# A two-block transformer kernel: masks and softmax factors of the attention moved to TensorE, and the first block run in three passes over the tokens

## The chip, the cores and the metric

The kernel runs on one core of a Trainium2 chip. A core has TensorE (PE, matrix products), VectorE (DVE), ScalarE (ACT), GpSimd (POOL), SyncE (SP), and 16 DMA engines that they share. Times are device microseconds of one execution; lower is better. All data are fp32.

## What is computed

512 tokens (four tiles of 128) of width 1024 go through two blocks. The first has 16 extra meta tokens in front. Cut to what matters here:

```python
h = concatenate([meta, x])                       # 16 + 512 tokens
z = rmsnorm(h) @ w_in                            # latents, retention q k v g, two gates
y_a = mla_branch(...)                            # causal attention, 8 heads, keys of 64+32
y_r = retention_branch(...)                      # chunks of 128 with a carried state
h = h + (sigmoid(za) * y_a + sigmoid(zr) * y_r) @ w_mix_out
# experts: 8 heads x 16 picks of 16384 for each token
act = gelu(einsum('td,tkd->tk', x, peer_u[idx])) # idx from two top-16 lists of 128 keys
h = h + einsum('tk,tkd->td', gates * act, peer_v[idx])
```

The second block has a pooled branch, an attention of 16 heads with three branches for each head (compressed keys, selected keys, window; the last two are plain causal here), a merge of both, and an MLP of width 4096. A score row is masked causally, `p = softmax(s)`; each branch is multiplied by a gate that belongs to the token and head. Where a token sees no compressed key, that branch is zero.

## The kernel before

**Passes.** The first block runs in passes over groups of tiles, `FIRST = ((0, 2), (2, 4))` at line 38: tiles 0 and 1 with the meta tokens, then tiles 2 and 3. The second block runs over `SECOND = ((0, 2), (2, 3), (3, 4))`. Each pass streams all weights of its block from memory through `weight_ring`, three slabs of up to 2 MB, in the order of `weight_plan`; SyncE issues a load as soon as the slab three places earlier has been used. `first_wave` writes the stages of a pass: norm (`n1`), latents (`lat`, `nq`, `nkv`), up-projections (`up`), head norms with rope (`qk`), turns (`tq`, `tk`), attention (`ma`), retention products and stage (`rp`, `tr`, `re`, `rn`), the gated merge (`m1`), output (`mix`), norm (`np`), the experts' queries (`pq`), and for each tile the selection of its experts (`sel0` to `sel3`). With several tiles in a pass, `merge_stage` and `product_stage` compute features by tokens; with one tile, `merge_tile_stage` and `turned_stage` compute tokens by features with 512 columns and turn the result. A slab that serves one tile is 8 products of 512 columns.

**The picks.** `Picks` gathers the expert rows. A step is one pick k of one tile t in one table: 4 tiles x 2 tables x 128 picks = 1024 steps, and each gathers 128 rows of 4 KB from `peer_u` or `peer_v` by an indirect DMA that GpSimd issues (line 315) into one of 8 buffers `picks_rows`. VectorE multiplies a `peer_u` row block with the tokens and sums (line 374), or adds a weighted `peer_v` row block to `h` (line 380). For tile 1, three of four `peer_v` picks are added by TensorE instead, with a diagonal of weights that GpSimd makes (lines 333 and 403). The gathers of tile t can start when its expert numbers are written (line 1465). `SHARES` says how many steps VectorE does within each stage, spread evenly between its own instructions: `g.picks.use(dve)`. The order of all engines is thus fixed when the program is written. A tile's picks must be done before the second block uses the tile (`finish`); `drain_0` takes what is left of tiles 0 and 1. Up to there 512 steps have been done: 24 in `sel1`, 358 in the pass over tiles 2 and 3, 51 each in `sel2` and `sel3`, 28 in the drain.

**Attention.** `attention_stage` works on pairs of items; an item is one head (and branch) of one tile. For a pair s: TensorE computes scores into PSUM (line 863, meta keys at 865); VectorE adds the mask and takes the row's least in one instruction, which also writes the masked scores back to PSUM (line 945, scores are negated); ScalarE takes the exponential and its sum (907); VectorE forms 1/sum (954) and multiplies the probabilities by it and by the gate (956, 958; for compressed keys also by the table `cmp_seen`, 953); TensorE turns each block of 128 keys against the identity (874); ScalarE copies them out (917, 920); TensorE multiplies by the values (885). On TensorE the order is scores of pair s, turns of s - 1, values of s - 2. Each item has its own semaphore counts for `least` and `normed`. In the second block a triple of pairs (compressed, selected, window) serves two heads, so 8 triples a tile.

## Time and profile before

| | |
|---|---|
| median of 3 runs | 3163.65 us (3157.81 to 3178.35) |
| profiled execution | 3159.39 us, of which span 3158.1 us |
| PE busy | 2272.4 us (72%) |
| DVE busy | 1802.2 us (57%) |
| POOL busy | 1432.2 us (45%) |
| ACT busy | 426.0 us (13%) |
| DMA | 829.57 MB, of which 539.99 MB gathered |
| granted TensorE clock, mean | 0.81 |

The page slices the span in 40 parts of 79 us: TensorE's busy share is high in the first 470 us and in the last 500 us, GpSimd's only from 525 to 2750 us, and the DMA engines' share is 0.7 or more from 710 to 2770 us. The shares of busy time are averages over stages with different limits, so the stages are read one by one. TensorE's records are pipelined, so its busy time is not its speed. It runs at one of two clocks, 1.2 or 2.4 GHz; the granted share of a stretch is the mean, 0.50 for all at the lower and 1.00 for all at the higher.

### The profile page before, as it was taken

The numbers are of one execution on the slowest core, as the hardware profiler recorded it, in microseconds if no ns is written. First come the engines' busy times: TensorE is split into PE (matmuls) and PEld (weight loads), VectorE is DVE, ScalarE is ACT, GpSimd is POOL, SyncE is SP. The second block draws the span as 40 slices with busy tenths as digits, with TensorE's granted clock in tenths as the row PEclk, the third lists the DMA queues.
The fourth block names the chain that finished last, engine by engine and source line by source line (L and its number), as shares of the span: only waits on it lengthen the run. The fifth ranks groups of instructions, "written<-read, shape, count | busy, mean of one in ns | idle before, by whom it ended". The sixth has DMA issues, their size and how long they took to land. (4 is left out here: it accounts for less than half of the span.)

```text
span 3158.1 us, 24727 instructions
## 1 busy us (share of the span) xinstructions
PE 2272.4 (72%) x8222; PEld 1376.0 (44%) x8222; DVE 1802.2 (57%) x3876; ACT 426.0 (13%) x1209; POOL 1432.2 (45%) x1137
## 2 busy tenths in 40 slices
PE   5997980056673784767674478979957687969989
PEld 3535850023432662322344235758425443437544
DVE  1512119978779677566477897674666854224300
ACT  1212000011200100000000232012000321013310
POOL 0000002377667787778767764676655433100000
PEclk9796995577695796999885557989977688987999
DMA  3310522599889999978889877999998779942376
GB/s 129 121 67 27 173 96 101 157 350 370 282 337 329 333 401 352 321 237 266 293 306 398 288 249 230 394 386 393 363 360 330 259 246 379 340 153 83 126 259 220
DMA packets 291759, 829.57 MB, mean 263 GB/s; under 512 B 23568, under 2 KB 30016, under 8 KB 290864
## 3 DMA queue, kind: packets, MB, share of 16 engines
q0 software_dynamic: 148464, 539.99, 47.7%
q1 hardware_dynamic: 139872, 283.19, 24.7%
q10 hardware_dynamic: 3296, 4.80, 0.4%
q8 instruction: 66, 1.08, 0.1%
q14 instruction: 61, 0.50, 0.1%
HBM read 825.81 MB, written 2.10 MB: 262 GB/s over the span
## 5 line engine op out<-in xcount | busy, mean ns | idle before, releaser
L315 POOL DMA_INDIRECT picks_rows<-peer_u_dram,expert x512 | 723.5, 1413 | 830.2 <-DVE expert L1465 516.2
L315 POOL DMA_INDIRECT picks_rows<-peer_v_dram,expert x512 | 618.1, 1207 | 477.4 <-DVE h L380 354.6
L374 DVE CUSTOM_DVE_ANT_0 picks_rows<-picks_rows,xn 128x1024 f32<-128x1024 f32 x512 | 613.7, 1223 | 169.0 <-DMA picks_rows<-peer_u_dram,expert 144.4
L380 DVE SCALAR_TENSOR_TENSOR h<-picks_rows,picks_weight,h 128x1024 f32<-128x1024 f32 x416 | 535.0, 1286 | 189.4 <-DMA picks_rows<-peer_v_dram,expert 116.3
L465 PE MATMUL psum<-weight_ring,hnT 128*128 128x512 f32 (+4 forms) x576 | 236.9, 573 | 23.0 <-DMA weight_ring<-w_in_dram 10.9
L403 PE MATMUL psum<-picks_rows,picks_diag 128*128 128x512 f32 x384 | 187.3, 625 | 59.9 <-POOL picks_diag L333 59.5
L1753 PE MATMUL psum<-weight_ring,aT 128*128 128x512 f32 x512 | 220.8, 593 | 3.1 <-ACT aT L2060 1.4
L465 PEld LDWEIGHTS psum<-weight_ring,hnT 128*128 128x128 f32 (+1 forms) x576 | 106.2, 187 | 152.4 <-issue 137.5
L874 PE MATMUL psum<-identity_sb,na_probs 128*128 128x128 f32 (+2 forms) x384 | 93.7, 359 | 100.9 <-DVE na_probs L958 79.4
L656 PE MATMUL psum<-identity_sb,n_scaled 128*128 128x128 f32 (+1 forms) x104 | 24.1, 412 | 181.9 <-DVE n_scaled L640 181.9
L1753 PEld LDWEIGHTS psum<-weight_ring,aT 128*128 128x128 f32 x512 | 96.9, 190 | 125.3 <-issue 120.5
L403 PEld LDWEIGHTS psum<-picks_rows,picks_diag 128*128 128x128 f32 x384 | 67.8, 194 | 178.1 <-issue 176.2
L465 PE MATMUL psum<-weight_ring,mergedT 128*128 128x512 f32 x256 | 117.2, 620 | 20.1 <-DVE mergedT L1216 18.7
L1333 PE MATMUL psum<-weight_ring,xn 128*128 128x512 f32 x256 | 117.1, 613 | 11.2 <-DVE xn L621 7.4
L1181 PE MATMUL psum<-hnT,weight_ring 128*128 128x256 f32 x512 | 116.4, 390 | 5.0 <-ACT xn L1140 5.0
L465 PE MATMUL psum<-xn,weight_ring 128*128 128x256 f32 x512 | 113.2, 385 | 8.6 <-DVE xn L621 8.6
L874 PEld LDWEIGHTS psum<-identity_sb,na_probs 128*128 128x128 f32 (+2 forms) x384 | 48.4, 159 | 161.7 <-DVE na_probs L958 152.4
L907 ACT ACTIVATE na_probs<-psum,na_least 128x15 f32<-128x15 f32 (+6 forms) x192 | 83.7, 441 | 190.9 <-DVE na_least L945 190.8
L1181 PEld LDWEIGHTS psum<-hnT,weight_ring 128*128 128x128 f32 x512 | 100.3, 196 | 20.1 <-ACT xn L1140 5.8
L465 PEld LDWEIGHTS psum<-xn,weight_ring 128*128 128x128 f32 x512 | 98.9, 193 | 22.8 <-issue 8.9
L1770 DVE TENSOR_TENSOR h<-h,psum 128x512 f32<-128x512 f32 x8 | 5.5, 689 | 180.9 <-PE psum L1753 180.9
L945 DVE CUSTOM_DVE_ANT_0 psum<-psum,mask_sb 128x128 f32<-128x128 f32 (+7 forms) x160 | 76.4, 514 | 51.9 <-PE psum L865 31.3
(353 smaller groups left out, 3170.8 us busy)
## 6 DMA issues: line engine op xcount, KB each, us to landing
weight_ring<-w_ff_dram SPq DMA_DIRECT2D x48, 2048.0 KB, 11.0
weight_ring<-w_in_dram SPq DMA_DIRECT2D x44, 2048.0 KB, 13.6
weight_ring<-w_proj_nsa_dram SPq DMA_DIRECT2D x6, 2048.0 KB, 8.1
weight_ring<-w_out_dram SPq DMA_DIRECT2D x6, 2048.0 KB, 14.8
weight_ring<-w_ret_out_dram SPq DMA_DIRECT2D x4, 2048.0 KB, 8.0
weight_ring<-w_mix_out_dram SPq DMA_DIRECT2D x4, 2048.0 KB, 18.9
weight_ring<-w_peer_q_dram SPq DMA_DIRECT2D x4, 2048.0 KB, 13.4
picks_rows<-peer_u_dram,expert POOLq DMA_INDIRECT x512, 7.8
```

What stands on the lines that cost most here:

```text
L315: pool.indirect_dma_start(out=self.rows[:, n % GATHERS, :], out_offset=None, in_=table, in_offset=bass.IndirectOffsetOnAxis(ap=self.expert ...
L374: ins = nc.vector.tensor_tensor_reduce(out=row, in0=row, in1=self.x[t], scale=1.0, scalar=0.0, op0=ALU.mult, op1=ALU.add, accum_out=self.d ...
L380: ins = nc.vector.scalar_tensor_tensor(out=h, in0=row, scalar=self.weight[:, t % 2, k:k + 1], in1=h, op0=ALU.mult, op1=ALU.add)
L403: mm = nc.tensor.matmul(self.g.psum[:, bank, :], self.diag[:, at % DIAGS, :], self.rows[:, n % GATHERS, 512 * c:512 * c + 512], start=(k = ...
L465: mm = g.nc.tensor.matmul(g.psum[0:rows, n % BANKS, 0:cols], lhsT, rhs, start=(k == 0), stop=(k == len(pairs) - 1))
L656: mm = nc.tensor.transpose(g.psum[:, 2 * (t % 2) + c // 4, P * (c % 4):P * (c % 4) + rows], buffer(t)[0:rows, P * c:P * c + P], g.identity ...
L874: mm = nc.tensor.transpose(turned(j, m, keys), probs[:, j % 4, at:at + keys], g.identity[:])
L907: nc.scalar.activation(probs[:, i % 4, 0:items[i].keys], scores(i), ACT.Exp, bias=least[:, i % 8:i % 8 + 1], scale=-1.0, accum_out=rowsum[ ...
L945: nc.vector.tensor_tensor_reduce(out=scores(i), in0=scores(i), in1=items[i].mask, scale=1.0, scalar=-LOWEST, op0=ALU.add, op1=ALU.min, acc ...
L1181: mm = nc.tensor.matmul(g.psum[0:rows, n % BANKS, 0:cols], lhsT, rhs, start=(k == 0), stop=(k == len(pairs) - 1))
L1333: mm = nc.tensor.matmul(g.psum[:, n % 3, :], lhsT, rhs, start=(k == 0), stop=(k == len(pairs) - 1))
L1753: mm = nc.tensor.matmul(g.psum[:, n_tiles * b + t, :], aT[:, KT * k + i, P * t:P * t + P], w[:, i, :], start=(k == 0 and i == 0), stop=(k ...
```

## The change

**The passes.** `FIRST` becomes ((0, 1), (1, 2), (2, 4)). Tile 0 and the meta tokens go alone, then tile 1 alone, then tiles 2 and 3. The weights of the first block are streamed three times. `sel0` ends pass 0, `sel1` pass 1. The shares are 140 steps up to and with `sel1` (121 and 19), 241 in the pass over tiles 2 and 3, 34 and 35 in `sel2` and `sel3`, 62 in the drain. The shares of the second block stay.

**The attention.** The mask is added by TensorE: after both scores of a pair, a product of the identity and the mask of the last 128 keys (the only ones that can be masked) is accumulated in PSUM. VectorE takes the least of both items in one `tensor_reduce` without writing scores back; the reciprocals of the pair are one instruction, the gates another. For items of more than 128 keys VectorE no longer scales the probabilities but writes `turner`, a diagonal of the factors, for both items, and TensorE turns the blocks by a full product with that diagonal in place of the turn against the identity. Items of up to 128 keys are scaled, both in one instruction. `cmp_seen` is replaced by zeroing gates of tile 0 once at the start. The signals `least` and `normed` count pairs, no longer items.

```diff
-FIRST = ((0, 2), (2, 4))
+FIRST = ((0, 1), (1, 2), (2, 4))
 SHARES = {
-    "sel1": 24, "n1_1": 13, "lat_1": 13, "nq_1": 9, "nkv_1": 9, "up_1": 12, "qk_1": 16, "tq_1": 6, "tk_1": 5, "ma2_1": 26,
+    "n1_1": 5, "lat_1": 5, "nq_1": 3, "nkv_1": 3, "up_1": 4, "qk_1": 7, "tq_1": 1, "tk_1": 2, "ma1_1": 10, "rp_1": 13,
...
+        turner = sb("turner", [P, 4, P]) if widest > P else None
...
-                mm = nc.tensor.matmul(scores(i)[:, 0:it.kT.shape[-1]], it.q, it.kT, start=True, stop=True)
+                n = it.kT.shape[-1]
+                nc.tensor.matmul(scores(i)[:, 0:n], it.q, it.kT, start=True, stop=False)
+            for i in pair(s):
+                it = items[i]
+                n, masked = it.kT.shape[-1], it.mask.shape[-1]
+                mm = nc.tensor.matmul(scores(i)[:, n - masked:n], g.identity[:], it.mask, start=False, stop=True)
...
-                pe.wait_ge(*s_normed.after(j + 1))
+                it = items[j]
+                pe.wait_ge(*s_normed.after(s + 1))
...
+                    if it.by_turn:
+                        mm = nc.tensor.matmul(turned(j, m, keys), probs[:, j % 4, at:at + keys], turner[:, j % 4, :], start=True, stop=True)
+                    else:
+                        mm = nc.tensor.transpose(turned(j, m, keys), probs[:, j % 4, at:at + keys], g.identity[:])
...
-                act.wait_ge(*s_least.after(i + 1))
+                act.wait_ge(*s_least.after(s + 1))
...
-                for i in pair(s):
-                    dve.wait_ge(*s_scores.after(i + 1))
-                    nc.vector.tensor_tensor_reduce(out=scores(i), in0=scores(i), in1=items[i].mask, scale=1.0, scalar=-LOWEST,
-                                                   op0=ALU.add, op1=ALU.min, accum_out=least[:, i % 8:i % 8 + 1]).then_inc(s_least.sem, 1)
+                it = items[2 * s]
+                dve.wait_ge(*s_scores.after(2 * s + 2))
+                nc.vector.tensor_reduce(least[:, both(s, 8)], both_scores(s), AX_X, ALU.min).then_inc(s_least.sem, 1)
                 g.picks.use(dve)
...
+                f = factor[:, both(s, 8)]
+                dve.wait_ge(*s_exp.after(2 * s + 2))
+                link(nc.vector.reciprocal(f, rowsum[:, both(s, 8)]))
+                if it.gate is not None:
+                    link(nc.vector.tensor_tensor(f, f, it.gate, ALU.mult))
+                if it.by_turn:
+                    if s >= 2:
+                        dve.wait_ge(*s_turned.after(2 * s - 2))
+                    ins = nc.vector.tensor_tensor(turner[:, both(s, 4), :], g.identity[:].unsqueeze(1).to_broadcast([P, 2, P]),
+                                                  f.unsqueeze(2).to_broadcast([P, 2, P]), ALU.mult)
+                else:
+                    p = probs[:, both(s, 4), 0:it.keys]
+                    ins = nc.vector.tensor_tensor(p, p, f.unsqueeze(2).to_broadcast([P, 2, it.keys]), ALU.mult)
+                ins.then_inc(s_normed.sem, 1)
```

How the rows of the engines move is shown at three places. The first is VectorE where the expert numbers of tile 0 are written (`expert<-`). Before, the selection of tile 1 follows (`sel_best`), with picks (`picks_dots`) already between:

```order
L1465 SCALAR_TENSOR_TENSOR expert<-sel_number 128x128
L1469 TENSOR_REDUCE sel_total<-sel_weight 128x8
L1470 RECIPROCAL sel_inverse<-sel_total 128x8
L1471 TENSOR_TENSOR gates_sb<-sel_weight,sel_inverse 128x128
L1428 MAX sel_best<-psum 128x8 x4
L374 ISA picks_rows,picks_dots<-picks_rows,xn 128x1024
L374 ISA picks_dots 128x1
L1428 MAX sel_best<-psum 128x8 x4
```

Of the change, the same place; it comes at row 175 of VectorE's order in place of row 284:

```order
L1496 SCALAR_TENSOR_TENSOR expert<-sel_number 128x128
L1500 TENSOR_REDUCE sel_total<-sel_weight 128x8
L1501 RECIPROCAL sel_inverse<-sel_total 128x8
L1502 TENSOR_TENSOR gates_sb<-sel_weight,sel_inverse 128x128
L632 MEMSET n_1_sums 128x1
L634 TENSOR_SCALAR n_1_mean<-n_1_sums 128x1
L636 RECIPROCAL n_1_inverse<-n_1_root 128x1
L645 TENSOR_SCALAR n_1_scaled<-h,n_1_inverse 128x1024
L379 ISA picks_rows,picks_dots<-picks_rows,xn 128x1024
```

The whole pass over tile 1, from its norm (`n_1`) on, now stands behind the first expert numbers and among the picks.

The second place is VectorE in the attention of tile 1 in the second block (`na_0`), a pair of 256 keys between picks (the rows that add to `h`). Before:

```order
L945 ISA psum,na_0_least<-psum,mask_sb 128x256
L945 ISA na_0_least 128x1
L945 ISA psum,na_0_least<-psum,mask_sb 128x256
L945 ISA na_0_least 128x1
L380 SCALAR_TENSOR_TENSOR h<-picks_rows,picks_weight,h 128x1024
L954 RECIPROCAL na_0_factor<-na_0_rowsum 128x1
L958 TENSOR_SCALAR na_0_probs<-na_0_probs,na_0_factor,branch_gates_0 128x256
L954 RECIPROCAL na_0_factor<-na_0_rowsum 128x1
L958 TENSOR_SCALAR na_0_probs<-na_0_probs,na_0_factor,branch_gates_0 128x256
```

Of the change:

```order
L973 TENSOR_REDUCE na_0_least<-psum 128x2
L385 SCALAR_TENSOR_TENSOR h<-picks_rows,picks_weight,h 128x1024
L977 RECIPROCAL na_0_factor<-na_0_rowsum 128x2
L979 TENSOR_TENSOR na_0_factor<-na_0_factor,branch_gates_0 128x2
L983 TENSOR_TENSOR na_0_turner<-identity_sb,na_0_factor 128x256
```

Eight instructions of the pair have become four.

The third place is TensorE in the attention of tile 3 (`na_2`), one triple. Before:

```order
L863 MATMUL psum<-nsa_kT_sb,qT_2 128x512 x2
L874 MATMUL psum<-identity_sb,na_2_probs 31x128 x2
L863 MATMUL psum<-nsa_kT_sb,qT_2 128x512 x2
L874 MATMUL psum<-identity_sb,na_2_probs 128x128 x8
L885 MATMUL psum<-na_2_probsT,v_cmp_sb 64x128 x2
L863 MATMUL psum<-k_cmpT_sb,qT_2 128x31 x2
L874 MATMUL psum<-identity_sb,na_2_probs 128x128 x8
L885 MATMUL psum<-na_2_probsT,nsa_kv_sb 64x128 x8
```

Of the change:

```order
L881 MATMUL psum<-nsa_kT_sb,qT_2 128x512 x2
L885 MATMUL psum<-mask_sb,identity_sb 128x128 x2
L898 MATMUL psum<-na_2_turner,na_2_probs 128x128 x8
L911 MATMUL psum<-na_2_probsT,v_cmp_sb 64x128 x2
L881 MATMUL psum<-k_cmpT_sb,qT_2 128x31 x2
L885 MATMUL psum<-cmp_mask_sb,identity_sb 128x31 x2
L898 MATMUL psum<-na_2_turner,na_2_probs 128x128 x8
L911 MATMUL psum<-na_2_probsT,nsa_kv_sb 64x128 x8
```

Each pair has gained two mask products behind its scores, and its eight turns have the same place with another right-hand side (`na_2_turner`).

## Rows read from the trace of the kernel before

**Rows 1.** Instructions on the tile `expert` (duration ns min/median/max, first and last start):

```profile
L315 POOL DMA_INDIRECT picks_rows<-peer_u_dram,expert x512: 933/1494/3326, 524.8 to 2341.0; - x171
```

**Rows 2.** Instructions on the tile `h`, same columns:

```profile
L380 DVE SCALAR_TENSOR_TENSOR h<-picks_rows,picks_weight,h x416: 1268/1283/1512, 800.8 to 2777.2; 128x1024 f32<-128x1024 f32 x139
```

**Rows 3.** VectorE's groups by shape, 1757 to 1942 us (busy us, mean ns):

```profile
L380 DVE SCALAR_TENSOR_TENSOR h<-picks_rows,picks_weight,h 128x1024 f32<-128x1024 f32 x71 | 90.9, 1280 | 0.2 <-issue 0.2
L374 DVE CUSTOM_DVE_ANT_0 picks_rows<-picks_rows,xn 128x1024 f32<-128x1024 f32 x17 | 20.8, 1221 | 3.5 <-DMA picks_rows<-peer_u_dram,expert 3.5
L954 DVE RECIPROCAL na_factor<-na_rowsum 128x1 f32<-128x1 f32 x96 | 14.9, 156 | 1.6 <-ACT na_probs L907 1.6
L945 DVE DVE_READ_ACCUMULATOR2_ANT na_least<- 128x1 f32 x96 | 13.4, 148 | 0.0
L958 DVE TENSOR_SCALAR na_probs<-na_probs,na_factor,branch_gates 128x256 f32<-128x256 f32 x32 | 13.2, 412 | 1.2
L945 DVE CUSTOM_DVE_ANT_0 psum<-psum,mask_sb 128x256 f32<-128x256 f32 x32 | 12.9, 445 | 0.0
...
L374 DVE DVE_READ_ACCUMULATOR2_ANT picks_dots<- 128x1 f32 x17 | 1.4, 82 | 0.0
```

**Rows 4.** Stretches of the first block: length, busy us by engine, granted clock, DMA share, GB/s:

```profile
24.00:121.00 97.00, 84.63 (x269) 45.38 (x270) 43.55 (x94) 13.50 (x33) 0.00 (x0) 0.95 0.36 125
121.00:167.00 46.00, 43.82 (x184) 29.96 (x184) 13.49 (x64) 16.28 (x67) 0.00 (x0) 0.59 0.01 2
167.00:246.00 79.00, 78.40 (x176) 29.00 (x176) 10.25 (x20) 6.45 (x12) 0.00 (x0) 0.98 0.20 67
246.00:300.00 54.00, 37.69 (x176) 28.63 (x176) 17.70 (x60) 12.50 (x37) 0.00 (x0) 0.59 0.11 39
300.00:400.00 100.00, 98.46 (x448) 86.13 (x448) 10.11 (x24) 8.08 (x20) 0.00 (x0) 0.98 0.40 137
400.00:470.00 70.00, 61.38 (x210) 41.18 (x210) 9.99 (x18) 5.32 (x10) 0.00 (x0) 0.90 0.29 100
470.00:525.00 55.00, 1.98 (x32) 1.78 (x32) 52.23 (x208) 1.59 (x2) 0.24 (x1) 0.54 0.03 11
525.00:609.00 84.00, 3.78 (x32) 3.52 (x32) 79.45 (x257) 0.31 (x1) 35.58 (x32) 0.52 0.62 200
609.00:1273.00 664.00, 401.36 (x1431) 268.03 (x1432) 524.34 (x827) 79.78 (x192) 483.19 (x356) 0.74 0.92 339
1273.00:1532.00 259.00, 188.64 (x449) 73.04 (x447) 150.78 (x455) 4.26 (x7) 215.01 (x217) 0.95 0.81 276
```

**Rows 5.** Stretches: merge of tiles 2 and 3, first block; of tile 2, second block:

```profile
1052.00:1153.00 101.00, 100.14 (x448) 87.03 (x448) 63.67 (x116) 7.58 (x18) 73.27 (x52) 0.97 0.98 369
2563.00:2615.00 52.00, 50.91 (x116) 22.25 (x116) 11.95 (x12) 4.16 (x6) 9.68 (x7) 0.96 0.83 304
```

**Rows 6.** Timeline of TensorE, one 2 MB slab for one tile (start us, us):

```profile
2661.47 7.03 PE L1333 MATMUL psum<-weight_ring,xn 128*128 128x512 f32 x16
```

**Rows 7.** Stretches: second block's attention, tiles 0 and 1, tile 2, tile 3:

```profile
1758.00:1942.00 184.00, 117.04 (x576) 61.37 (x576) 171.08 (x520) 63.66 (x297) 117.30 (x92) 0.54 0.81 264
2464.00:2563.00 99.00, 74.19 (x433) 45.68 (x433) 86.33 (x244) 41.79 (x148) 41.11 (x37) 0.74 0.69 213
2876.00:2961.00 85.00, 74.09 (x529) 50.08 (x528) 54.02 (x208) 48.78 (x147) 0.00 (x0) 0.89 0.00 1
```

**Rows 8.** VectorE's reduces by shape, whole span (busy us, mean ns):

```profile
L1464 DVE TENSOR_REDUCE sel_number<-sel_scratch 128x128 f32<-128x2048 f32 x8 | 18.3, 2286 | 0.3
L789 DVE TENSOR_REDUCE qk_head_sums<-qk_head_squares 128x8 f32<-128x768 f32 x8 | 7.6, 953 | 0.3
```

**Rows 9.** Timeline of TensorE in the attention of tile 3 (start us, us):

```profile
2885.37 1.12 PE L874 MATMUL psum<-identity_sb,na_probs 128*128 128x128 f32 x8 [0.50 <-ACT na_probsT L917]
2886.42 1.58 PE L885 MATMUL psum<-na_probsT,nsa_kv_sb 128*64 128x128 f32 x16
2887.93 1.13 PE L863 MATMUL psum<-nsa_kT_sb,qT 64*128 64x512 f32 x4
```

55 lines of the change are left out of this document (27 added, 28 removed), and 12 rows, old and new, of the table SHARES.

## The prediction

> **What bounds the kernel now.** I read first when the instructions on two tiles start and end, then the groups of one engine by shape, then the busy times of stretches. The gathers of expert rows start at 524.8 us and not before, because they wait for the first expert numbers [rows 1]; the last row is added at 2777.2 us [rows 2], and 381 us of tile 3 alone follow. Between lie 1024 gathers, 540 MB in all (0.527 MB each), and VectorE pays 1.22 us (1.30 with the read of its accumulator) for each of `peer_u` and 1.28 us for each of `peer_v` [rows 3]. So the span has three parts: 525 us without gathers, 2252 us with them, 381 us after.
>
> In the first 525 us TensorE is nearly always busy at full clock and the DMA share is 0.01 to 0.40; in the last 55 us VectorE alone picks the experts [rows 4]. In the pass over tiles 2 and 3 (609 to 1273 us) nothing is full alone: VectorE 524 of 664 us, TensorE 401, DMA share 0.92 [rows 4]. In the gating stage of it TensorE has 100 of 101 us and the DMA share is 0.98 at 369 GB/s [rows 5], which I take as the most that the DMA engines give. From 1273 to 1532 us GpSimd is busiest, 215 of 259 us, with the gathers and diagonals of tile 1 [rows 4].
>
> **Part 1: the first block in three passes.** The gathers come earlier, and a third pass over the block's weights is read. By the plan's shapes a pass is 5792 columns of `w_in` at 4 KB plus 16.9 MB of others, 40.6 MB.
>
> The start. Pass 0 now has tile 0 and the 16 meta rows. From [rows 4]: 97 us become 64 (products of a tile or the meta rows against a slab fall from 19 to 11, the norms shrink a little), 46 become 27 (8 of 16 heads), 79 become 50 (7 of 11 products), 54 become 33 (one retention chunk instead of two), 100 become 52 (the same seven slabs' worth in the one-tile form took 52 us [rows 5]; a 2 MB slab is 16 instructions in 7.0 us [rows 6]), 70 become 45, and the selection stays at 55. With the 24 us of loading: 350 us, so the gathers start 175 us earlier. Nothing else uses the DMA then; 40.6 MB in 326 us is 125 GB/s, hidden.
>
> The pass over tile 1. Without picks it would take pass 0's 271 us less the meta rows' products and a meta unit of norms (35 us), 236. It carries 121 picks, 157 us of VectorE at 1.30. How these add I take from the pass of before: without picks, 446 us of pass 0 (24 to 470), less the meta rows, plus the longer attention, about 435; with 358 picks (465 us of VectorE) it took 664. That is 0.74 of the two added. So 0.74 x (236 + 157) = 290 us. The DMA has to move 40.6 + 121 x 0.527 = 104 MB: 282 us at 369 GB/s, 307 at the mean 339 of the pass of before [rows 4]. I take 305, near the DMA's end. Selection of tile 1 with 19 picks instead of 24: 84 - 5 x 1.3 = 77.
>
> The pass over tiles 2 and 3 carries 241 picks: 0.74 x (435 + 313) = 554. Some stages there stand at the gathers' pace and give back all of a removed pick, so I take 545. DMA is no bound: 168 MB, 455 us at 369 GB/s. Then selections 2, 3 and the drain hold 131 picks, 130 before: GpSimd is the bound there, 260 us as before.
>
> Sum: 350 + 305 + 77 + 545 + 260 = 1537 us, against 1532 now: **+5**. The 175 us won at the start, the 7 of a lighter selection and 119 of a lighter pass over tiles 2 and 3 are paid back by 305 of an extra pass.
>
> **Part 2: the attention.** Per pair of heads VectorE had, at 256 keys, 2 x (0.445 + 0.148 + 0.156 + 0.412) = 2.3 us [rows 3]. Now: one reduce over 512 elements, which from 953 ns at 768 and 2286 at 2048 is 1.04 ns an element plus 0.15, 0.68 us [rows 8]; a reciprocal and a product of two columns, 0.16 each; and a diagonal of 128x256, which I price at 0.42 by the scaling of 256 columns. That is 1.42, 0.62 of before. With fewer keys the fixed parts of the eight or ten removed instructions weigh more, and I take 0.52 over all. In the attention of tiles 0 and 1 VectorE has 171 of 184 us [rows 7], 113 of them on picks [rows 3]; so 58 become 30, 28 us less.
>
> TensorE pays for it. In the attention of tile 3 at full clock, 8 blocks are turned in 1.05 us, 16 instructions of values take 1.5 and two heads' scores 1.1 (by the starts of the rows, 1.13 by the last one's own time) [rows 9]: 3.6 us a pair, 8.4 a triple with the compressed pair, of 85/8 = 10.6. A full product of 128 columns takes two instructions of 0.11 (7.03/16 for 512 columns, a quarter [rows 6]), 0.22 us, against 0.13 for a turn. So the masks add 0.44 a pair, the turns as products 0.7 to 0.9, the small pair 0.2: 2.7 us, 11.1 a triple, with the clock already 0.89. VectorE no longer hides anything here (54 of 85 us, no picks). The factor is now also made after both exponentials. 8 x 11.1 = 89 plus 8 for filling and for waits: **97 us, +12**. Bounds: 0 (if only today's idle is used) and +22.
>
> Tiles 0 and 1: VectorE 171 to 143, plus 10 for steps that have no pick between the reduce and the factor, so that the wait for two exponentials shows. TensorE gets 24 us more at full clock, 45 at the granted 0.54, 117 + 45 = 162 [rows 7]. The later of the two with some waits is 169: **-15**; bounds -41 (VectorE alone) and 0. Tile 2: VectorE 86 to about 66, TensorE 74 + 25 = 99 at its clock of 0.74, somewhat less if the clock rises: **-5**, bounds -14 and +5. The first block's attention: less VectorE, more TensorE at a low clock, no net, contained in the passes.
>
> **Sum:** 3159.4 (the profiled execution, 1.3 us more than its span) + 5 + 12 - 15 - 5 = 3156. The profiled execution lies 4 us under the median 3163.65 of the three. I predict 3152, leaning a little to the faster rivals: no change that 1% can tell, and 1% (32 us) is about what a measurement of this kernel tells from no change.
>
> **Rivals.**
> The clock (17%). From 121 to 167 us TensorE is busy 44 of 46 us and yet has 0.59 of its clock, the tiles 0 and 1 attention 0.54 at 117 of 184, the tile 3 attention 0.89 at 74 of 85 [rows 4, 7]. What runs there is short: turns and small products. If replacing turns by products and adding masks lifts the stretches from 1.2 to mostly 2.4 GHz, VectorE bounds tiles 0 and 1 (148 us, -36, where waits shrink too), tile 2 comes to 85 (-14), tile 3 to 95 (+10), and the attention of the first block gives 20: 3159 + 5 - 60 = 3104. The Trainium skill, "TensorE: Matmul & The Clock Gate", Part 4, says that transposes do not count as busy for the gate as matmuls do; by that rule this is what happens. The 0.89 with a quarter of the work in turns neither proves nor excludes it.
>
> Passes that pack better (15%): tile 1 at the DMA's end, 283, and the next pass at 505, because picks hide fully once they are fewer: 3156 - 23 - 40 = 3093.
>
> Passes that pack worse, slower than before (24%): the shares are few per stage, and the one-tile stages are chains. A pick placed between a norm and its drain adds its whole 1.3 us. If a removed pick gives back only what it added on average, (664 - 435)/358 = 0.64 us, the pass over tiles 2 and 3 takes 589 and that over tile 1 313: 3156 + 44 + 8 = 3208. It decides (slower by over 1%) from about 583 us on for the pass over tiles 2 and 3.
>
> The earlier start is nothing (4%): if pass 0 waits for slabs; then its DMA share would be high. The one-tile stretch moved 304 GB/s with TensorE busy 51 of 52 us [rows 5], against it.
>
> The forecast has 40%, its own range 3120 to 3190. Faster by over 1% (under 3132) comes from the first two rivals and a little of the forecast, 0.33; slower (over 3195) 0.24; the rest 0.43. The range 3085 to 3212 takes in the rivals' centres and leaves out about a fifth.
>
> **What would show it.** First gather at 340 to 360 us; expert numbers of tile 1 about 382 us later; tile 1's last pick near 1537; the pass over tiles 2 and 3 between 520 and 570 us; the attention stretches 169, 94 and 97 us, with TensorE's busy time up in all and VectorE's down by a third in the last. Wrong would be a first gather after 400 us, a granted clock over 0.8 in the attention of tiles 0 and 1, or a tile 3 attention under 85 us. A DMA share under 0.8 in the pass over tile 1 would say that its chains bound it, not its bytes.

## The result

| | median | against the kernel before |
|---|---|---|
| kernel before | 3165.26 us (15 runs, 3156 to 3182) | |
| changed kernel | 3192.61 us (15 runs, 3182 to 3209) | 1.009, 95% interval 1.0069 to 1.0111 |

The change costs about 28 us, where 3152 us (0.4% faster) had been forecast. The time is inside the wide range of the prediction (3085 to 3212), but outside the forecast's own 3120 to 3190 and on the wrong side of no change. The profiled executions differ by as much: the span grew from 3158.1 to 3186.3 us. As the change intends, TensorE's busy time rose from 2272.4 to 2382.6 us and VectorE's fell from 1802.2 to 1731.2; the mean granted clock rose from 0.81 to 0.83.

### The profile after

First gather, last pick of the kernel, and the two sums that close tile 1's picks, by tile (duration ns min/median/max, first and last start in us); they answer to [rows 1] and [rows 2]:

```profile
L320 POOL DMA_INDIRECT picks_rows<-peer_u_dram,expert x512: 934/1314/3227, 352.2 to 2344.0; - x171
L385 DVE SCALAR_TENSOR_TENSOR h<-picks_rows,picks_weight,h x416: 1264/1283/1530, 687.7 to 2784.5; 128x1024 f32<-128x1024 f32 x139
L433 DVE TENSOR_TENSOR h<-h,psum x2: 678/682/686, 1551.6 to 1552.2; 128x512 f32<-128x512 f32 x2
```

Before, the last of these rows read:

```profile
L428 DVE TENSOR_TENSOR h<-h,psum x2: 679/684/689, 1541.3 to 1541.9; 128x512 f32<-128x512 f32 x2
```

The gathers start 173 us earlier, and yet tile 1 is complete 10.3 us later. Stretches of the changed kernel, columns as in [rows 4] and [rows 7]: pass 0 up to its attention, what follows that, the selection of tile 0; the pass over tile 1; its selection; the pass over tiles 2 and 3; their selections and the drain; below the gap the first block's attention of tile 0, of tile 1, of tiles 2 and 3, and the second block's of tiles 0 and 1, of tile 2 and of tile 3:

```profile
24.00:87.00 63.00, 49.71 (x147) 24.35 (x147) 25.20 (x59) 8.35 (x21) 0.00 (x0) 0.92 0.52 182
118.00:297.00 179.00, 155.85 (x408) 70.00 (x407) 24.38 (x57) 20.71 (x41) 0.00 (x0) 0.87 0.45 157
297.00:352.00 55.00, 2.06 (x32) 1.86 (x32) 51.88 (x206) 1.88 (x3) 0.00 (x0) 0.54 0.03 10
352.00:652.00 300.00, 200.67 (x573) 105.64 (x574) 182.65 (x346) 39.40 (x95) 168.15 (x126) 0.75 0.94 345
652.00:735.00 83.00, 11.94 (x61) 6.40 (x59) 68.78 (x229) 5.46 (x8) 21.44 (x23) 0.61 0.57 180
735.00:1275.00 540.00, 389.06 (x1505) 262.04 (x1506) 380.79 (x571) 75.93 (x187) 312.82 (x237) 0.82 0.84 301
1275.00:1542.00 267.00, 198.55 (x478) 80.32 (x476) 151.83 (x457) 5.03 (x9) 216.91 (x220) 0.94 0.82 274
...
87.00:118.00 31.00, 27.83 (x113) 17.65 (x114) 4.31 (x13) 8.14 (x34) 0.00 (x0) 0.60 0.06 24
431.00:462.00 31.00, 30.07 (x144) 22.30 (x144) 16.97 (x34) 9.45 (x34) 13.67 (x12) 0.72 0.87 311
866.00:960.00 94.00, 70.89 (x384) 50.76 (x384) 64.24 (x66) 23.59 (x68) 55.72 (x43) 0.85 0.73 253
1773.00:1944.00 171.00, 146.33 (x832) 102.37 (x830) 146.32 (x289) 64.29 (x296) 107.98 (x87) 0.66 0.82 271
2470.00:2573.00 103.00, 89.43 (x625) 67.52 (x626) 73.44 (x132) 42.49 (x147) 37.10 (x37) 0.87 0.65 200
2883.00:2987.00 104.00, 98.12 (x752) 74.52 (x752) 36.66 (x96) 50.24 (x148) 0.00 (x0) 0.97 0.00 1
```

From first to last instruction of each, the second block's attention stages now take 171.6, 102.9 and 103.8 us, against 184.3, 98.8 and 85.1. In every one VectorE works less, TensorE works more and has more of its clock; only the first got shorter. The sum of the three is +10.1, tile 1's end is +10.3, and 7.8 us are spread over stages that the change does not touch.

Timeline of TensorE in tile 3's attention, answering to [rows 9] (start us, us):

```profile
2902.18 1.13 PE L881 MATMUL psum<-nsa_kT_sb,qT 64*128 64x512 f32 x4
2903.24 0.71 PE L885 MATMUL psum<-mask_sb,identity_sb 128*128 128x128 f32 x4
2904.17 2.05 PE L898 MATMUL psum<-na_turner,na_probs 128*128 128x128 f32 x16 [0.22 <-DVE na_turner L983]
2906.15 0.43 PE L911 MATMUL psum<-na_probsT,v_cmp_sb 31*64 31x128 f32 x4
```

The eight turns of a pair, 1.05 us from start to start before, are 16 instructions and 1.98 us (2904.17 to 2906.15).

### The profile page after: what moved, and what is told of

Read it like the earlier page. It is cut to its first block and busy times, and to the rows that moved or that the text cites. A ratio compares the mean times of both kernels' runs of the same rounds, so it can differ in the third digit from the quotient of the medians.

```text
span 3186.3 us, 25522 instructions
## 1 busy us (share of the span) xinstructions
PE 2382.6 (75%) x8814; PEld 1428.5 (45%) x8814; DVE 1731.2 (54%) x3341; ACT 444.4 (14%) x1227; POOL 1399.6 (44%) x1137
## 3 DMA queue, kind: packets, MB, share of 16 engines
q8 instruction: 71, 1.16, 0.1%
## 5 line engine op out<-in xcount | busy, mean ns | idle before, releaser
L320 POOL DMA_INDIRECT picks_rows<-peer_u_dram,expert x512 | 703.7, 1374 | 737.9 <-DVE expert L1496 343.6
L320 POOL DMA_INDIRECT picks_rows<-peer_v_dram,expert x512 | 608.5, 1189 | 609.5 <-DVE h L385 463.8
L661 PEld LDWEIGHTS psum<-identity_sb,n_scaled 128*128 128x128 f32 (+1 forms) x104 | 19.7, 222 | 239.4 <-issue 202.5
L1321 DVE TENSOR_TENSOR m_term<-psum,m_gates 128x512 f32<-128x512 f32 x16 | 11.1, 692 | 193.1 <-PE psum L1293 193.1
L898 PE MATMUL psum<-na_turner,na_probs 128*128 128x128 f32 x576 | 85.7, 304 | 32.3 <-DVE na_turner L983 27.2
L470 PE MATMUL psum<-weight_ring,h2T 128*128 128x512 f32 (+1 forms) x256 | 97.2, 541 | 6.6 <-DVE kc_sb L1566 5.1
L898 PEld LDWEIGHTS psum<-na_turner,na_probs 128*128 128x128 f32 x576 | 75.5, 209 | 39.7 <-DVE na_turner L983 34.2
```

The source lines that it names most:

```text
L320: pool.indirect_dma_start(out=self.rows[:, n % GATHERS, :], out_offset=None, in_=table, in_offset=bass.IndirectOffsetOnAxis(ap=self.expert ...
L470: mm = g.nc.tensor.matmul(g.psum[0:rows, n % BANKS, 0:cols], lhsT, rhs, start=(k == 0), stop=(k == len(pairs) - 1))
L661: mm = nc.tensor.transpose(g.psum[:, 2 * (t % 2) + c // 4, P * (c % 4):P * (c % 4) + rows], buffer(t)[0:rows, P * c:P * c + P], g.identity ...
L898: mm = nc.tensor.matmul(turned(j, m, keys), probs[:, j % 4, at:at + keys], turner[:, j % 4, :], start=True, stop=True)
```

## The experiments

Each ran beside the kernel before on the same chip, and each ratio is to that, with its 95% interval. The number of a kernel is that in its label. Each stage length is read from one profiled execution. The theory after reading the two traces was that both parts of the change lose some 10 us each.

### The two parts alone, and the attention taken apart

Kernel 1 is the changed one with `FIRST` and `SHARES` of before; kernel 2 is the one before with

```diff
-FIRST = ((0, 2), (2, 4))
+FIRST = ((0, 1), (1, 2), (2, 4))
```

and the new shares. Kernels 3 and 4 have two passes, and of the attention only TensorE's mask products with the pair's reduce, or only the diagonals. Both choose in one function, the first line in kernel 3 and the second in kernel 4 (`mask_pe` and `factors` of every stage):

```diff
+    return (True, "each")
```

```diff
+    return (False, "turner")
```

> The two passes and the shares of before, with the whole new attention. Theory (the parts add up, and both lose): the second block's attention moves as in the changed kernel, -13 us for tiles 0 and 1, +4 for tile 2, +19 for tile 3, and the first block's attention by nothing that shows, so +10 us, 3175. Rival 1 (the passes are the loss, and the attention would win on its own): between -10 and 0. Rival 2 (the attention is the whole loss, through the first block too, where two of its three stages stand among picks): +24 to +30, with tile 1's last pick 10 us later than the 1532 us of before.

> The three passes and the shares of the change, with the attention of before. Theory: +10 us at tile 1's last pick (1542), and 3 to 4 more in the second block's first stages, as in the changed kernel, so +12 us, 3177. Rival 1 (passes are the whole loss): +20 to +28. Rival 2 (the new attention is what makes the passes late): 0 to +3, with the last pick of tile 1 at 1532 to 1535.

> The two passes of before; of the attention only TensorE's masks and the one reduce for a pair, while VectorE scales each item as before and the blocks are turned against the identity. By rows, a pair's masks cost TensorE about 0.5 us and VectorE loses 0.5 us of 2.3 at 256 keys. Theory: tiles 0 and 1 -7 us, tile 2 0, tile 3 +7 (8 triples by 0.9 us), sum 0 to +3. Rival (the wait for both scores and both exponentials is the loss, not TensorE's work): tile 3 +12 or more here, and little in the run with the diagonals alone. The clock: if turns against the identity are what keeps the granted clock low, the attention of tiles 0 and 1 stays at 0.54 here; if it is how much TensorE has to do, it rises to about 0.6.

> The two passes of before; of the attention only the diagonals of factors and the full products with them (items of up to 128 keys scaled in one instruction), while VectorE adds the masks and takes the least item by item as before. By rows, the eight turns of a pair take 1.98 us in place of 1.05, 1.9 us for each of 8 triples of tile 3. Theory: tiles 0 and 1 -5 us, tile 2 +3, tile 3 +12, sum +10, so most of the attention's loss is here. Rival (the masks are the loss): tile 3 under +5. The clock: if turns against the identity are what keeps it low, the attention of tiles 0 and 1 rises from 0.54 to 0.66 or more here; if it is how much TensorE has to do, to about 0.6, as with the masks alone.

| kernel | median | ratio | interval | us |
|---|---|---|---|---|
| attention alone | 3204.38 | 1.0118 | 1.0086 to 1.0151 | +37 |
| passes alone | 3155.68 | 0.9967 | 0.9947 to 0.9986 | -10 |
| masks alone | 3178.31 | 1.0034 | 1.0009 to 1.0058 | +11 |
| diagonals alone | 3162.34 | 0.9981 | 0.9962 to 1.0 | -6 |

The theory fell for both parts. The passes gain, and the attention is the whole loss: +37 and -10 make the +28 of the change. It fell for the halves of the attention too: the masks alone cost 11 us where 0 to 3 were expected, and the diagonals alone, expected to be most of the loss at +10, gain 6. The size of the attention's loss surprised, since the second block's stages give only +10. The first stage of the first block, tiles 0 and 1 without any picks, shows the rest. It took 46.3 us before ([rows 4], 121 to 167). With the whole new attention, and below it with the diagonals alone:

```profile
121.00:186.00 65.00, 62.26 (x256) 42.65 (x256) 9.36 (x24) 16.35 (x67) 0.00 (x0) 0.61 0.01 3
```

```profile
119.00:184.00 65.00, 62.25 (x224) 39.95 (x223) 11.52 (x48) 18.02 (x67) 0.00 (x0) 0.52 0.01 2
```

TensorE has 62 of 65 us and little over half of its clock; nothing else is near full. The stage is TensorE's alone, so it has no idle time that would take up added products, and their price goes by the clock that the stage gets. In the changed kernel this is spread over its passes. Beside the passes alone, tile 0's stage goes from 21.9 to 30.3 us, tile 1's from 29.1 to 31.3, tiles 2 and 3's from 86.0 to 94.0: 18.6 us, of which 14.6 arrive where tile 1 is complete, since with the passes alone that comes at 1537.0:

```profile
L430 DVE TENSOR_TENSOR h<-h,psum x2: 680/684/689, 1537.0 to 1537.6; 128x512 f32<-128x512 f32 x2
```

For the second block the two halves of the attention are told apart stage by stage (us, from first to last instruction):

| stage | before | masks alone | diagonals alone | both (changed kernel) |
|---|---|---|---|---|
| tiles 0 and 1 | 184.3 | 178.0 | 175.3 | 171.6 |
| tile 2 | 98.8 | 105.2 | 94.3 | 102.9 |
| tile 3 | 85.1 | 100.0 | 91.5 | 103.8 |

In tile 3 the kernel with the masks loses more, +15 and not the +7 expected; the diagonals lose 6 there and not 12. Timeline of TensorE with the masks alone, and then with the diagonals alone, one triple each; the first rows of each stand one triple apart:

```profile
2895.98 1.58 PE L921 MATMUL psum<-na_probsT,nsa_kv_sb 128*64 128x128 f32 x16
...
2898.55 0.71 PE L895 MATMUL psum<-mask_sb,identity_sb 128*128 128x128 f32 x4
2899.10 1.04 PE L910 MATMUL psum<-identity_sb,na_probs 128*128 128x128 f32 x8
...
2900.77 0.63 PE L895 MATMUL psum<-cmp_mask_sb,identity_sb 128*128 128x31 f32 x4
2902.63 1.12 PE L910 MATMUL psum<-identity_sb,na_probs 128*128 128x128 f32 x8 [1.23 <-ACT na_probsT L953]
...
2907.11 1.58 PE L921 MATMUL psum<-na_probsT,nsa_kv_sb 128*64 128x128 f32 x16
```

```profile
2898.98 1.58 PE L921 MATMUL psum<-na_probsT,nsa_kv_sb 128*64 128x128 f32 x16
...
2901.90 2.05 PE L908 MATMUL psum<-na_turner,na_probs 128*128 128x128 f32 x16 [0.28 <-DVE na_turner L1014]
...
2909.79 1.58 PE L921 MATMUL psum<-na_probsT,nsa_kv_sb 128*64 128x128 f32 x16
```

A triple takes 11.13 us with masks and 10.81 with diagonals. Before, it took 9.51:

```profile
2889.32 1.58 PE L885 MATMUL psum<-na_probsT,nsa_kv_sb 128*64 128x128 f32 x16
...
2894.88 1.12 PE L874 MATMUL psum<-identity_sb,na_probs 128*128 128x128 f32 x8 [1.18 <-ACT na_probsT L917]
...
2898.83 1.58 PE L885 MATMUL psum<-na_probsT,nsa_kv_sb 128*64 128x128 f32 x16
```

So masks add 1.6 us and diagonals 1.3, and the changed kernel has 12.4: the sum. A wait of 1.2 us for ScalarE's copy stands in each triple before, and still stands there with the masks. The copy stands on ScalarE behind the exponentials of the next pair, and these wait for the least, which waits for the scores. The head of this chain, before and then with the masks alone (the scores before start at 2887.93 us [rows 9]):

```profile
2889.09 0.70 DVE L945 CUSTOM_DVE_ANT_0 psum<-psum,mask_sb 128x512 f32<-128x512 f32 x1 [1.84 <-PE psum L863]
2889.89 0.69 ACT L907 ACTIVATE na_probs<-psum,na_least 128x512 f32<-128x512 f32 x1 [2.47 <-DVE na_least L945]
```

```profile
2905.19 1.13 PE L887 MATMUL psum<-nsa_kT_sb,qT 64*128 64x512 f32 x4
2906.99 1.23 DVE L984 TENSOR_REDUCE na_least<-psum 128x2 f32<-128x1024 f32 x1 [2.52 <-PE psum L895]
2908.25 0.69 ACT L943 ACTIVATE na_probs<-psum,na_least 128x512 f32<-128x512 f32 x1 [3.69 <-DVE na_least L984]
```

From the scores to the first least it is 1.80 us in place of 1.16, with the mask products of both items between. From the least to the first exponential it is 1.26 us in place of 0.80, because one reduce now gives the least of both items; before, the exponential of the first item could start while VectorE took the least of the second. The triple has this second step twice in its chain (again 2899.30 to 2900.56, where it was 2892.03 to 2892.81 before). So of the 1.6 us some 0.6 come from the mask products and 0.9 from the common reduce. The rival of kernel 3, that waiting for both items is the loss and not TensorE's work, was right for the larger part of it. No kernel has the masks without the common reduce, so this split is read from one triple and was not tested. The diagonals do fill the wait for the copy (0.28 us of another wait left), which is why 1.9 us more of products cost 1.3.

### Which block, and which stages

Kernel 5 has the new attention in the first block's stages alone, kernel 6 only in the second block's stage of tiles 0 and 1, both with two passes. Kernel 7 has the three passes and chooses by stage:

```diff
+    return {"na2_0": (True, "turner"), "na2_1": (False, "turner")}.get(tag, (False, "each"))
```

> The two passes of before; the new attention in the first block's three attention stages only, the second block's as before. In the run with the whole new attention, the attention of tiles 0 and 1 in the first block, where TensorE has 62 of 65 us at 0.61 of its clock, took 65.1 us against 46.3, and the two stages of tiles 2 and 3 124 against 119. Theory (the first block's attention, which I had priced at nothing, is the larger part of the loss): +19 to +25 us, so 3187, with tile 1's last pick at 1553. Rival (it lies in the second block: the run with all of it ended 15 us later by more than its start): +5 or less, since what is lost in the first 525 us is caught up while the gathers run.

> The two passes of before; the new attention only in the second block's attention of tiles 0 and 1, where VectorE has 171 of 184 us; all other attention stages as before. Theory (there VectorE bounds, and its relief reaches the end of the kernel): the stage 184 to 172 us, the kernel -12 us, 3153. Rival (what the stage gains is given back behind it, because the gathers, 0.81 of the DMA's time there, set the pace of the picks up to 2777 us): -3 to +2.

> The three passes and shares of the change; the new attention only in the second block's attention of tiles 0 and 1, there the diagonals alone for tile 2, and the attention of before for tile 3 and the whole first block. Theory (gains of stages add up): -10 by the passes, -12 for tiles 0 and 1, -4 for tile 2, so -26 us, 3139. Rival (they do not add up, since both relieve the same gathers): -10 to -15, 3152.

Measured were 3188.37 us for the first block alone (1.009, 1.0073 to 1.0107, +28), 3150.03 for tiles 0 and 1 of the second (0.997, 0.9954 to 0.9986, -9), and 3142.93 chosen by stage (0.9948, 0.9935 to 0.9961, -16). The first block is thus some three quarters of the attention's loss. It arrives before the second block starts: with kernel 5 tile 1 is complete 30 us later than before (1541.3):

```profile
L436 DVE TENSOR_TENSOR h<-h,psum x2: 680/684/689, 1571.3 to 1571.9; 128x512 f32<-128x512 f32 x2
```

The expected 1553 and +19 to +25 us were too low. The cause is TensorE's own work there; groups of TensorE in kernel 5's first stage (x instructions, busy us, mean ns):

```profile
L908 PE MATMUL psum<-ma_turner,ma_probs 128*128 128x128 f32 x48 | 15.4, 458 | 2.2 <-DVE ma_turner L1014 2.2
L895 PE MATMUL psum<-mask_sb,identity_sb 128*128 128x128 f32 x32 | 10.1, 415 | 0.0
L908 PE MATMUL psum<-ma_turner,ma_probs 128*16 128x128 f32 x32 | 9.3, 392 | 0.0
```

Before, the two kinds of turn took 8.2 and 6.4 us; now 24.7, plus 10.1 for masks: 20 us more, of the 23.5 by which the stage grew (46.3 to 69.8). The gain of tiles 0 and 1 does reach the end: in kernel 6's profile the stage takes 177 us, 7 less than before (12 less were expected), and the kernel gains 9. Passes (-10), tiles 0 and 1 (-9) and tile 2 (-4) add up to -23 where -16 was measured, with an interval of -20 to -12. That lies between the theory and its rival, and the parts' own intervals (-17 to -4, -15 to -4) are too wide to say whether gains are lost in adding up.

### Where the drain's time comes from

Kernel 8 is the three passes alone with 22 picks moved out of the drain (only the shares that change are shown); kernel 9 is kernel 7 with fewer diagonals at the end of tile 1:

```diff
-"qk_1": 7, "rp_1": 13, "nq_2": 6, "qk_2": 12, "ma3_2": 18, "tr_2": 5, "drain_0": 62
+"qk_1": 12, "rp_1": 15, "nq_2": 9, "qk_2": 18, "ma3_2": 22, "tr_2": 7, "drain_0": 40
```

```diff
-    return t == 1 and k % 4 > 0
+    return t == 1 and k % 4 > (0 if k < 64 else 1)
```

> The three passes with the attention of before, and 22 picks taken from the drain (62 to 40), where a pick takes 1.86 us and GpSimd has 0.88 of the time, and given to stages of the passes where VectorE stands idle for 0.24 to 0.5 of the time (5 and 6 to the head norms, 3 to the latent's norm, 2 to the retention products, 4 to the attention of tile 3, 2 to the retention's turns). Theory (the picks hide there, the drain gets shorter by 41 us): -15 to -30 us against the three passes alone, 3133. Rival 1 (those stages are chains, and a pick between two links adds its whole 1.3 us): -12 to -5, 3146. Rival 2 (the gathers' bytes are the pace everywhere, 1.43 us for 0.527 MB at 369 GB/s): within 5 us of the three passes alone.

> As the run chosen by stage, but of tile 1's last 64 picks from peer_v, nearly all of them in the drain, TensorE adds every second in place of three of four, so VectorE adds 16 more and GpSimd makes 16 diagonals fewer. In the drain of that run GpSimd issues a gather in 1.09 us and makes a diagonal in 0.79, with 0.2 between: 1.88 us a pick, and a pick takes 1.86. Theory (GpSimd sets the pace of the drain): 16 x 0.79 = 12 us less up to tile 1's last pick, VectorE at 0.32 of its time has room; the kernel -12 us against the run chosen by stage, 3130. Rival (the weights and gathers set the pace, DMA share 0.86 at 286 GB/s there): within 3 us of it.

Kernel 8 took 3157.28 us, 0.9988 (0.9976 to 1.0001). By the ratios that is 6 us more than the passes alone, with intervals that overlap, so it can't be told from no change: against the theory and the first rival, and near where the second rival put it. The drain, from the expert numbers of tile 3 to the end of tile 1, did get 37 us shorter (1429.1 to 1537.0 us with the passes alone, 1465.6 to 1536.4 in kernel 8). But these expert numbers come 36.5 us later, so the drain ended where it had. A moved pick cost 1.7 us at its new place (36.5/22), more than VectorE's own 1.3: idle time of VectorE in those stages was no free room. Whether the gathers' bytes are the reason, as the second rival says, was not tested. Kernel 9 took 3140.97 us, 0.9939 (0.9919 to 0.9959), level with kernel 7 within the intervals: the rival, and not the 12 us of the theory. In its profile tile 1 was complete at 1539.1 us, in kernel 7's at 1532.1; kernel 10, with the drain of kernel 7, has 1539.3, so these 7 us say nothing. GpSimd from 1412 to 1522 us, first in kernel 7, then in kernel 9:

```profile
L325 POOL DMA_INDIRECT picks_rows<-peer_v_dram,expert x59 | 64.3, 1090 | 12.0 <-issue 11.9 <-PE psum L413 0.2
L343 POOL TENSOR_SCALAR picks_diag<-identity_sb,picks_weight 128x128 f32<-128x128 f32 x44 | 35.4, 804 | 1.5
```

```profile
L325 POOL DMA_INDIRECT picks_rows<-peer_v_dram,expert x55 | 65.8, 1196 | 19.9 <-PE psum L413 10.2 <-issue 9.7
L343 POOL TENSOR_SCALAR picks_diag<-identity_sb,picks_weight 128x128 f32<-128x128 f32 x27 | 26.1, 967 | 0.9
```

With 16 more picks on VectorE each gather issue and each diagonal takes longer (1090 to 1196 ns, 804 to 967), and GpSimd waits 10 us for TensorE where it had waited 0.2, while TensorE's granted clock falls from 0.97 to 0.83. The prediction had called GpSimd the bound of the drain; the number of its instructions alone does not set this pace, and what does was not settled.

### The clock in the first block's attention

The diagonals alone measured -6 us in the median, yet their profiled execution was the slowest of twelve, 3174 us, and has the 65 us stage. Does the clock in that stage differ between executions of one kernel? Kernel 10 puts a wide product ahead of each pair's scores in the first block's stages of tile 0 and of tile 1, and is kernel 7 otherwise:

```diff
+                if tag in ("ma0_0", "ma1_1") and i == 2 * s:
+                    nc.tensor.matmul(g.psum[:, i % 4, :], g.identity[:], g.filler, start=True, stop=True)
```

Kernels 11 and 12 split kernel 5 into diagonals and masks; 13, 14 and 15 are the kernel before, kernel 5 and kernel 11 again, one execution each.

> As the run chosen by stage, but in the first block's attention of tile 0 and of tile 1 TensorE does one extra product of 128x512 ahead of each pair's scores, which is overwritten: work that nothing needs, 4 for each stage. Tile 0's stage takes 21.9 us there with TensorE busy 20.8 at 0.50 of its clock, tile 1's 29.8 us at 0.59. Theory (the small products alone keep the clock at its lower level however densely they stand, and wide ones lift it): granted clock over 0.8 in both, and the stages shorter by 3 to 6 us each in spite of the extra work. Rival (the clock stays low for the whole stage): tile 0's stage 4 x 1.7 us longer, 28 to 29 us, at 0.50.

> The two passes of before; in the first block's attention only the diagonals and the products with them, VectorE's masks kept; the second block as before. With diagonals in every stage the first one took 65.2 us (46.3 before) and the profiled execution 3174, but the median of its twelve was 3162, under the kernel before. Theory (the stage always stays at the lower clock and always loses): the stage at 63 to 68 us with a granted clock under 0.65, the kernel +17 to +24, 3183. Rival (when the clock comes back differs between executions, and the profiled one was unlucky): the stage anywhere from 45 to 65, the kernel's median +5 or less, its runs spread by 20 us or more.

> The two passes of before; in the first block's attention only TensorE's masks and the one reduce for a pair; scaling and turns as before, the second block as before. With masks in every stage the first one took 47.8 us (46.3 before). Theory (of the first block's loss of 28 us the diagonals are all): 0 to +3 us, 3163 against 3160. Rival (the masks cost as much as the diagonals, and the 47.8 us was a lucky clock, which had come back at 155 us there): the stage 55 us or more, the kernel +8 to +12.

> The kernel before, profiled once more, for the first block's attention of tiles 0 and 1 (46.3 us at 0.59 of the clock in the profile shown, 50.9 in the one other profile with that stage unchanged). Theory (whether the clock falls at the entry of this stage, and when it comes back, differs from execution to execution): another value from 32 to 51 us, with the granted clock the higher the shorter it is, and the kernel's time moving with it. Rival (the stage is the same each time): 46 to 51.

> The kernel with the whole new attention in the first block alone, profiled once more (69.8 us in the stage at the first look, 65.1 with the new attention everywhere). Theory (with both masks and diagonals the clock does not come back within the stage in most executions, which is why the pair costs 28 us and each part alone 10 or less): 64 to 70 us at 0.50 to 0.61. Rival (it is a draw here too): under 55 us.

> The kernel with the diagonals in the first block alone, profiled once more (65.2 and 65.3 us in the two profiles with this stage; the twelve times of this kernel lie in two groups, four at 3162 to 3164 and eight at 3172 to 3185). Theory (the groups are executions in which the clock holds in the stage and executions in which it does not): either 65 us and a kernel's time of 3172 or more, or a stage of 40 to 50 us and a time near 3163. Rival: 65 us in an execution near 3163.

Kernel 10 took 3142.77 us (0.994, 0.992 to 0.996), like kernel 7. Tile 0's stage took 28.1 us at 0.50, as the rival said. Tile 1's took 23.5 us at a granted clock of 1.00, where kernel 7 had 29.8 at 0.51, as the theory said; in the five three-pass kernels without wide products and with the old attention there (2, 7, 8, 9 and 16) the clock was 0.50 to 0.64. One of each, so wide products do not always lift the clock, and one execution does not show that they did in tile 1. Kernel 11 took 3174.12 us (1.002, 0.9999 to 1.0041), kernel 12 3162.81 (0.9987, 0.9963 to 1.0011) with runs from 3136 to 3175. Kernel 11's stage was as its theory had it (65.3 us at 0.52), but its time (+6 us, runs spread over 23) was near the rival's. Kernel 12's -4 us has an interval of -12 to +3, so it agrees with its theory that the masks cost nothing there, and its rival is out. The stage in every profile of a two-pass kernel:

| attention in that stage | us (span of that execution) |
|---|---|
| as before | 46.3 (3158), 50.9 (3164, kernel 6), 50.9 (3169) |
| masks | 47.8 (3178, masks everywhere), 33.9 (3154) |
| diagonals | 65.2 (3173, diagonals everywhere), 65.3 (3184), 51.9 (3157) |
| both | 65.1 (3199, both everywhere), 69.8 (3192), 71.0 (3196) |

Ten microseconds of this stage in kernel 12, in kernel 15, and in kernel 11, whose program is the same as kernel 15's:

```profile
131.00:141.00 10.00, 10.00 (x70) 7.48 (x68) 3.69 (x11) 3.54 (x18) 0.00 (x0) 1.00 0.01 2
```

```profile
151.00:161.00 10.00, 10.00 (x49) 6.89 (x49) 3.22 (x12) 4.10 (x16) 0.00 (x0) 0.74 0.00 0
```

```profile
151.00:161.00 10.00, 10.00 (x36) 6.52 (x34) 2.07 (x8) 2.71 (x10) 0.00 (x0) 0.50 0.00 0
```

At 1.00 of the clock (2.4 GHz) 70 instructions fall in 10 us, at 0.50 (1.2 GHz) 36, with TensorE busy for all 10 in both; the next ten microseconds of kernel 15 itself have 65, at 1.00. Kernels 11 and 15 do the same work at the same place of the program and differ by 13.4 us in the stage and by 26 in the kernel. They ran on different chips, but the twelve runs of kernel 11 on one chip also go from 3162 to 3185 us, the four shortest with a mean granted clock of 0.814 to 0.817 and the eight others with 0.809 to 0.815. So the moment at which the clock comes back differs between executions of one program, and this stage is very likely one source of the spread of its times. The kernel before gave 50.9 us again (kernel 13), which decides nothing between its theory and its rival. With both parts three of three executions stayed low until close to the end, at 0.54 to 0.61. That this is why the pair costs 28 us and each part alone -4 and +6 fits these profiles, but three are few, and it is not shown.

### The better kernel

Kernel 16 is kernel 7 without TensorE's masks anywhere:

```diff
+    return (False, "turner") if tag in ("na2_0", "na2_1") else (False, "each")
```

> As the run chosen by stage, but without TensorE's masks anywhere: the diagonals alone in the second block's attention of tiles 0 and 1 and of tile 2, all else as before, with the three passes. In tiles 0 and 1 both parts together took 175.8 us, the diagonals alone 175.3. Theory (VectorE's relief by the diagonals is all that this stage can use; the masks bring nothing in any stage): within 3 us of the run chosen by stage, 3142. Rival (the masks give another part of the gain, as they gave 6 us alone): +5 us or more, 3148.

It took 3137.85 us, 0.9934 (0.9912 to 0.9956): 21 us under the kernel before, by the two ratios some 49 under the changed one, and no slower than kernel 7 with its masks. Its second block's attention stages:

```profile
1754.00:1926.00 172.00, 107.28 (x639) 66.56 (x637) 153.01 (x437) 64.59 (x296) 114.67 (x88) 0.65 0.82 276
2450.00:2544.00 94.00, 71.50 (x528) 51.59 (x528) 75.72 (x204) 42.90 (x148) 38.30 (x37) 0.89 0.70 219
2854.00:2939.00 85.00, 74.34 (x528) 49.99 (x528) 54.03 (x208) 48.45 (x148) 0.00 (x0) 0.89 0.00 1
```

Both stages in which VectorE was nearly full gain (184 to 172, 99 to 94), and tile 3 keeps its 85 us.

## Why the prediction was wrong

**The passes.** Right in their parts: first gather 352.2 us for 350, the pass over tile 1 300 for 305, its selection 83 for 77, the pass over tiles 2 and 3 540 for 545, the rest 267 for 260. The passes alone bear it out: first gather at 345.6 us. In the pass over tile 1 the DMA share is 0.94 at 345 GB/s, above the 0.8 under which its chains were to be the bound; that its bytes bound it stays an argument. The 369 GB/s that the text took as the most the DMA engines give were not the most: the page of the kernel before has a slice of 79 us at 401. The +5 came out as +10, but that mixes two things: the passes by themselves brought tile 1 4 us earlier (1537.0 for 1541.3) and the kernel -10.

**The first block's attention: the step that failed.** The text put it at "less VectorE, more TensorE at a low clock, no net, contained in the passes". It has only a small cover of picks (none at all in tile 0), and in pass 0 [rows 4] had TensorE busy 43.8 of 46 us at 0.59: no idle time to absorb products, and the price of one twice that at full clock. The 40 turns and 0 mask products became 80 and 32, some 20 us by the groups above. Measured: 28 us with two passes, 18.6 of stages in the changed kernel, where the sum had 0. Without it the passes (-10) and the second block's attention (+9, the 37 of the whole less the 28 of the first block) would cancel. Neither half costs this much there by itself (kernel 12 -4, kernel 11 +6); why the pair costs 28 is open, apart from the added work and the clock that stayed low in all three profiles of it.

**Tile 3, +12 for +18.7.** The sign was right, and TensorE's added work was part of the cause; the size was not right. The triple was built from TensorE's instructions (8.4 us) plus the additions (2.7) to 11.1. But a triple took 9.5 at full clock, with 1.2 us of waiting in it, and this waiting stayed under the masks. The masks were priced by their columns at 0.44 and 0.2 us; start to start they are 0.55 a pair. The common reduce was counted only as a saving on VectorE, and it delays the exponentials by 0.45 us twice in a triple; masks and reduce together add 1.6. 9.5 + 1.6 + 1.3 is the 12.4 measured.

**Tile 2, -5 for +4.** VectorE's 86 of 99 us was taken as the bound. The diagonals alone bore that out (94.3), the masks turned it round (105.2). With both, TensorE has 89 of 103 us. My own second number, TensorE at 99 us at its old clock of 0.74, was nearer, and I argued it down with a rise of the clock. But the clock did rise, to 0.87, and the stage still took 103: that 99 was near is partly luck.

**Tiles 0 and 1, -15 for -12.7.** The size was right, partly by luck. The forecast took the later of two terms, TensorE's 162 us, with some waits. TensorE had 146 us, since its clock rose, and VectorE 146 (143 to 153 in the text). VectorE lost 25 us of work and the stage half of that, so VectorE stood idle for 25 us in place of 13. With the diagonals alone TensorE had 111 us and the stage took 175, so TensorE's work was not what held it.

**The clock.** That rival's premise came true in part: the granted share rose from 0.54 to 0.66, 0.74 to 0.87 and 0.89 to 0.97. In tiles 2 and 3 it rose with the diagonals alone (0.88, 0.95) and not with the masks alone (0.74, 0.90), which added work but kept the turns. In those two stages the traces agree with the Trainium skill, "TensorE: Matmul & The Clock Gate", Part 4, by which transposes do not count as busy for the clock as products do. In other stages they do not, and there the measurement decides. In tiles 0 and 1 of the second block the masks alone, with all turns kept, raised the clock more (0.54 to 0.64) than the diagonals alone (0.61), which the expectations of kernels 3 and 4 had named as the sign against this rule. In the first block's stage of tiles 2 and 3 both raised it alike (0.62 to 0.73 and 0.74), and in the first block's stage of tiles 0 and 1 kernel 12, which keeps the turns, had 1.00 for all of its 33 us. In kernel 5 that same stage, with products in the place of all turns, stood at 0.55 over 70 us, TensorE busy for 67, so the absence of turns did not lift it. In the second block's tiles 2 and 3 of the changed kernel the stages grew although the clock rose, so the clock did not give back what was added.

**The chances.** The rival on the slower side (24%) looked for the loss in picks packed badly. Nothing bore it out. There was no rival for the attention as a whole losing, though tile 3's bound of +22 and TensorE's share in [rows 4] spoke for one.

**The forecast as a number.** The terms add up to -3 us only. That it reads as 12 us under the median of before comes from two other things: the profiled execution lay 4 us under that median, and 4 to 5 us were taken off for the faster rivals.

## What to carry over

When work is moved from one engine to another, price it in every stage that runs the code, at the clock that stage has; where the receiving engine is busy for 95% of a stage, nothing takes up the added instructions, and their price can be twice as high in one execution as in another by the clock alone. Count a stage by its period (start to start of the repeated group) and not by the sum of the busy rows: a wait inside the period belongs to a chain, and work put at the head of that chain lengthens the period while work behind it may fill the wait. Joining two items in one instruction saves time on its engine, but what follows the first item now waits for the second as well; where the chain bounds, that is a loss. A code path that wins where one engine bounds and loses elsewhere should be chosen stage by stage: here that turned +28 us into -21.

## What the runs showed of the hardware

- The clock that TensorE gets in one stage differs between executions: 1.00 against 0.67 for the same instructions of this stage, 33.9 against 47.8 us (kernels 12 and 3, different chips), and 51.9 against 65.3 us for one program (kernels 15 and 11). In kernel 11 it stayed at 1.2 GHz from 131 to 181 us with TensorE busy throughout in the trace.
- At the low clock the turn of a block of 16 keys by a product with the diagonal takes nearly what one of 128 keys takes: 9.3 us busy for 32 instructions and 15.4 for 48 in kernel 5, 0.29 and 0.32 us each. The first block has such a block in every item.
- With extra 128x512 products between small ones the clock was 1.00 in one stage (23.5 us) and 0.50 in the other (28.1 us), one execution; without them it was 0.50 to 0.64 in the first and 0.50 in the second in five kernels.
- One reduce over two items of 512 columns took 1.23 us (masks alone). Before, mask and least took 0.70 and 0.73 us, one item each; the next exponential started 0.80 us after the first of them, and 1.26 us after the common reduce.
- With fewer picks on TensorE and more on VectorE, GpSimd's own instructions were longer, 804 to 967 ns for a diagonal and 1090 to 1196 for issuing a gather.
